# Loading the expert matrices of a hybrid decoder step as whole 4 MB transfers instead of 2 MB halves

## What is computed

```
def moe(x, w_router, b_router, w_gate, b_gate, w_up, b_up, w_down, b_down):
    logits = (x @ w_router + b_router)
    top_v, top_i = lax.top_k(logits, TOP_K)          # 4 of 32
    wts = softmax(top_v)
    ...
    g = xblk @ w_gate[eid] + b_gate[eid]
    u = xblk @ w_up[eid] + b_up[eid]
    g = minimum(g, 7.0); u = clip(u, -7.0, 7.0)
    hmid = (u + 1.0) * (g * sigmoid(1.702 * g))
    yblk = hmid @ w_down[eid] + b_down[eid]
```

## Time and profile before

| | before |
|---|---|
| device time, median of 3 runs | 1263.45 us (1262.87 to 1263.94) |
| the profiled execution's own time | 1263.72 us |
| span of its profile (first to last instruction) | 1262.0 us |
| PE busy | 1221.6 us (97%) |
| bytes moved | 455.83 MB, mean 361 GB/s |
| transfers of half matrices, 2048 KB each | 62 gate, 62 up, 62 down |

### The profile page before, as it was taken

How to read it: one execution, slowest core, us unless ns; L and a number is a source line. 1 busy time by engine, 2 the same in 40 slices (tenths; PEclk the granted TensorE clock), 3 DMA queues, 4 the chain that set the end, 5 groups by cost and what they waited for, 6 DMA issues and landing times.

```text
span 1262.0 us, 15821 instructions
## 1 busy us (share of the span) xinstructions
PE 1221.6 (97%) x6208; PEld 670.4 (53%) x6208; DVE 356.9 (28%) x958; ACT 225.9 (18%) x432; POOL 24.6 (2%) x53
## 2 busy tenths in 40 slices
PE   8999999999999999999999999999999999999998
PEld 6887778886444434354343444444343444434356
DVE  3423732236331212222121222222122231212136
ACT  2422422013111111111111101111111111111133
POOL 1000110001000000000000000000000000000000
PEclk9999999999999999999999999999999999999999
DMA  9742677745999999999999999999999999999980
GB/s 299 232 132 82 198 240 264 286 167 216 407 428 426 429 427 428 428 428 429 428 429 428 427 428 423 426 427 427 428 427 429 427 429 429 427 430 427 422 346 35
DMA packets 72668, 455.83 MB, mean 361 GB/s; under 512 B 7335, under 2 KB 41813, under 8 KB 47277
## 3 DMA queue, kind: packets, MB, share of 16 engines
q1 hardware_dynamic: 66192, 443.83, 85.7%
q0 software_dynamic: 2736, 9.08, 2.2%
q10 hardware_dynamic: 3692, 2.28, 0.7%
HBM read 449.33 MB, written 5.83 MB: 361 GB/s over the span
## 4 chain that ended last, share of the span: by engine, by line
PE 80%; DMA 16%; DVE 2%; ACT 1%; issue 0%; DVEq 0%; SPq 0%; ACTq 0%
PE bank L895 38%; PE bank L647 19%; DMA ring<-in_w_up_dram 11%; PE bank L911 5%; DMA ring<-in_w_gate_dram 5%; PE bank L930 4%; PE bank L968 3%; PE bank L1193 2%; PE bank L903 2%; PE bank L1069 2%; DVE regC L1653 1%; DVE regC L1635 1%; PE bank L689 0%; PE bank L918 0%; PE bank L786 0%
## 5 line engine op out<-in xcount | busy, mean ns | idle before, releaser
L895 PE MATMUL bank<-ring,regC 128*64 128x512 f32 x1984 | 437.8, 595 | 19.1 <-DVE regC L1653 11.3
L895 PEld LDWEIGHTS bank<-ring,regC 128*64 128x64 f32 x1984 | 138.1, 137 | 282.1 <-issue 256.2
L1635 DVE TENSOR_TENSOR regC<-bank,biasT 128x512 f32<-128x512 f32 x61 | 42.2, 692 | 591.6 <-PE bank L903 590.2
L895 PE MATMUL bank<-ring,xe_odd 128*64 128x512 f32 x896 | 198.4, 594 | 5.4 <-DMA ring<-in_w_up_dram 4.2
L647 PE MATMUL bank<-regA,ring 128*128 128x264 f32 x832 | 192.6, 388 | 0.0
L647 PEld LDWEIGHTS bank<-regA,ring 128*128 128x128 f32 x832 | 155.3, 190 | 30.8 <-issue 3.8
L895 PEld LDWEIGHTS bank<-ring,xe_odd 128*64 128x64 f32 x896 | 63.0, 137 | 128.9 <-issue 118.5
L911 PEld LDWEIGHTS bank<-regC,regB 128*128 128x128 f32 x816 | 95.9, 192 | 14.4 <-issue 13.5
L911 PE MATMUL bank<-regC,regB 128*128 128x128 f32 x816 | 100.7, 277 | 0.5 <-DVE hT L1671 0.3
L2091 ACT ACTIVATE regD<-bank 128x512 f32<-128x512 f32 x62 | 37.0, 597 | 241.5 <-PE bank L895 232.8
L1671 DVE TENSOR_TENSOR hT<-hT,bank 128x264 f32<-128x264 f32 x144 | 56.5, 426 | 74.7 <-PE bank L930 25.6
(11 more groups left out here) (346 smaller groups left out, 691.1 us busy)
## 6 DMA issues: line engine op xcount, KB each, us to landing
ring<-in_w_up_dram SPq DMA_DIRECT2D x62, 2048.0 KB, 24.8
ring<-in_w_down_dram SPq DMA_DIRECT2D x62, 2048.0 KB, 26.1
ring<-in_w_gate_dram SPq DMA_DIRECT2D x62, 2048.0 KB, 21.8
ring<-in_w_in_dram SPq DMA_DIRECT2D x28, 1024.0 KB, 7.0
out_dram<-ring POOLq DMA_DIRECT2D x9, 512.0 KB, 5.1
ring<-in_state_gla_dram POOLq DMA_DIRECT2D x8, 512.0 KB, 5.3
ring<-in_w_o_dram SPq DMA_DIRECT2D x4, 1024.0 KB, 7.5
ring<-in_w_gate_dram SPq DMA_DIRECT2D x4, 1024.0 KB, 28.7
```

The costliest lines, as they stand in the source:

```text
L895: ins = mm(bank[b][n * CAP:(n + 1) * CAP, :], lhs(k + i), by_k[s][:, i, n * 512:(n + 1) * 512], start=(k + i == 0), stop=(k + i == KT - 1))
L1635: return v.tensor_tensor(out, v_in, bias.to_broadcast([P, HALF, 2, CAP]), ALU.add)
```

## The change

For the experts at places 2 to 29 a matrix is now one transfer of 4 MB into two neighbouring slots. `by_pair` views slots 0 and 1, 2 and 3, 4 and 5, 6 and 7 as one place of two halves. SP issues it when both slots are free (it waits for one more used piece than the first half did before), and it raises the semaphore of the even slot alone. PE waits for that semaphore ahead of both pieces, so no matmul of a matrix starts before all 4 MB have landed. The experts at places 0, 1, 30 and 31 are loaded as before (`alone`). 84 transfers of 4 MB take the place of 168 of 2 MB. Each partition's 4 MB share is two runs of 16 KB, one from each half of the matrix, which lie 2 MB apart in memory.

```diff
+        by_pair = [view(ring, s * SLOT, 2, HALF * D) for s in range(0, SLOTS, 2)]
...
+        def alone(m):
+            return m < EARLY_EXPERTS * PER_EXPERT or m >= (E - (E - EARLY_EXPERTS) % UNROLL) * PER_EXPERT
+        def loader(m):
+            return m if alone(m) else m - m % 2
         def expert_loads(m):
-            return 16 * (m // SLOTS + 1)
+            m = loader(m)
+            return 16 * sum(n == loader(n) for n in range(m % SLOTS, m + 1, SLOTS))
...
+            def load_matrices(e, q, i):
+                for m in range(q * PER_EXPERT, (q + 1) * PER_EXPERT, 2):
+                    w = K3[m % PER_EXPERT // 2][0]
+                    sp.wait_ge(chunk_used, i * TURN + (m - SLOTS + 2))
+                    sp.dma_start(by_pair[m % SLOTS // 2], w[0, e].rearrange("(h p k) f -> p h (k f)", h=2, p=P))\
+                        .then_inc(slot_loaded[m % SLOTS], 16)
...
-                    load_expert(sp.value_load(order_i[0:1, bass.ds(i * UNROLL + (early + u), 1)], min_val=0, max_val=E - 1),
-                                early + u, i)
+                    load_matrices(sp.value_load(order_i[0:1, bass.ds(i * UNROLL + (early + u), 1)], min_val=0, max_val=E - 1),
+                                  early + u, i)
...
-                    return [(r % SLOTS, slot_loaded[r % SLOTS], i * loads + expert_loads(r), HALF * (r % 2))
+                    return [(r % SLOTS, slot_loaded[loader(r) % SLOTS], i * loads + expert_loads(r), HALF * (r % 2))
```

## The result

The changed kernel takes 1280.74 us (median of 4 runs, 1279.84 to 1281.61) against 1263.7 us before: 17.0 us more, a ratio of 1.0135 with a 95% interval of 1.0124 to 1.0147. Forecast were 1278.3 us and a range from 1271 to 1286.

A forecast was written before the change was run, and what follows sets the result against it. The weight stream at 428 GB/s was taken to set the expert part's time. 3.2 + 8.3 - 0.5 + 4.2 - 0.6 = +14.6 us on 1263.72 gave 1278.3 us, range 1271 to 1286.

The forecast's parts named there:

- A transfer's own cost: In the weight stream, 84 fewer transfers save between nothing and 6.7 us; 0.5 us taken for all.
- The lower bound: In the weight stream, fewer transfers save nothing, as packets fill 100.6% of sixteen engines with no rest between transfers.
- First gap: At the loop's first pair, pieces 12 and 13, the queue is empty and the later issue costs 3.2 us.
- Second gap: After the wide pass, entered 7.8 us later, the next matrix is issued too late and the stream loses 8.3 us.
- Waiting for the whole: At up of the loop's last expert, PE has both pieces to do after the pair lands: +4.2 us.
- the 0.6 made up: After the loop, PE's earlier wait of 0.56 us at 1176.84 is used up: -0.6 us.
- rival 5: TensorE's clock falls in PE's longer waits, some 6 us per pair of pieces; ten such give 1340 us; chance 3%.
- One reading of the prediction: Profile page before: DMA share 9 from eleventh slice to last but one, rate 423 to 430 GB/s from the twelfth.
- cheaper and slower transfers: Rivals on the 4 MB transfers: 0.08 us saved each, 1272.1 us, 10%; or stream 1.9% slower, 1293.9 us, 12%.
- That TensorE is the bound: Rival: TensorE bounds the kernel and the gaps vanish in its lead, 1263.7 us; chance 4%.

The follow-up runs named there:

- the two kernels with one rule each: Against the kernel before, 2 MB halves kept: issuing both when both slots are free, 1270.73 us; or PE waiting for both halves, 1273.73 us.
- the kernel with the rules alone: Against the changed kernel, two 2 MB transfers per matrix again, both issued when both slots are free, PE waiting for both halves: 1279.02 us.
- forty-two matrices that changed nothing: 4 MB transfers only at places 3 to 11 and 21 to 25, PE's program as in the kernel before: 1264.72 us, ratio 1.0004 to it.
- three matrices at place 2: 4 MB transfers only for the expert at place 2, PE's program as in the kernel before: 1266.53 us, ratio 1.0024 to it.
- the kernel with place 29 alone: Against the kernel before, 4 MB transfers only at place 29, PE waiting a second time ahead of every odd piece: 1268.61 us, ratio 1.0034.
- places 2 and 12 to 16: Against the kernel before, 4 MB transfers only there, in separate kernels, with a second PE wait ahead of odd pieces: 1270.13 and 1276.55 us.
- the four kernels that wait again ahead of every odd piece: 4 MB transfers at place 2, 12 to 16, 3 to 11 with 21 to 25, or 29, against the kernel before: 1270.13, 1276.55, 1270.17, 1268.61 us.
- the four with the same loop on SP and PE's old program: SP's loop written out; 4 MB transfers nowhere, at place 2, 12 to 16, or 3 to 11 with 21 to 25: 1264.18, 1266.53, 1272.47, 1264.72 us.
- the one with the wait rule alone: Against the kernel before, each half still issued when its slot is free, but PE waits for both halves ahead of the first piece: 1273.73 us.

## Why the prediction was right, and where its terms were off

The mechanism held at each step, and the range held the time. But every term that was off was off to the same side (by 0.5, 0.4, 0.6 and 1.7 us), so the forecast of 14.6 us was low. By the steps of the sum:

- *A transfer's own cost, 0.5 us saved.* Nothing was saved: 9.79 us a matrix against 2 x 4.90. The lower bound, no rest between queued transfers, was the true value, and a fixed part is paid only when the queue is empty: 12.9 and 13.1 us to landing at the two holes, where 12.6 was expected. With 9.79 us of moving, that is 3.1 and 3.3 us for a lone 4 MB transfer, not the 2.8 that was read from a lone 2 MB one.
- *First gap, 3.2 us.* 3.6: the issue was 0.1 later and the landing took 0.3 longer.
- *Second gap, 8.3 us.* 8.9. The wide pass began at 699.14 where 698.6 was worked out, the matrix left at 753.5 (753.0) and took 0.5 us longer to land. That it takes both rules to make this gap is shown by the two kernels with one rule each.
- *Waiting for the whole, 4.2 us; the 0.6 made up.* The 4.2 was too small by what the clock took. In the changed kernel's timeline of 1148 to 1245 the up matrix of the loop's last expert starts at 1159.66, 12.2 us after the 1147.48 of the earlier trace rows (11.0 forecast), and its second piece 5.87 us later instead of 4.2:

```profile
1159.66 5.35 PE L912 MATMUL bank<-ring,xe_odd 128*64 128x512 f32 x16 [3.24 <-DMA ring<-in_w_up_dram]
...
1165.53 3.65 PE L912 MATMUL bank<-ring,xe_odd 128*64 128x512 f32 x16
...
1230.17 7.09 PE L1086 MATMUL bank<-ring,regC 128*64 128x512 f32 x32 [1.38 <-DVE regC L1681]
```

The piece took 5.35 us instead of 3.65. The granted clock of the changed kernel around it:

```profile
1156.00:1168.00 12.00, 8.76 (x34) 2.78 (x34) 1.64 (x3) 1.23 (x2) 0.00 (x0) 0.86 0.99 423
```

That is the largest part of the sum that was missing: rival 5 named the clock, but as a case of its own with 3 in 100, and not as a term of the sum. Its idle time of 2.0 us per pair counted the transposes between up's pieces; gate's two pieces run back to back in 7.09 us, so the wait behind them is 9.79 - 7.09 = 2.7 us, and 3.24 here. Its price of tens of microseconds took ten pairs to run wholly at half clock. What the clock took is small, 5.35 - 3.65 = 1.7 us, since it came back within the piece (the transposes and the second piece behind it take their old 0.66 and 3.65); and it counts only here, where nothing behind it waits for the stream any more. It is not sure to come: with the wait of 2.70 us in the kernel with the rules alone it did not. With it, 3.6 + 8.9 - 0.3 + 4.2 + 1.7 - 0.6 = 17.5, where -0.3 is the difference between the two gaps added up (12.5) and the delay of the up matrix as PE meets it (12.2). From 1212.76 before to 1230.17 now are 17.4 us; the spans differ by 1279.8 - 1262.0 = 17.8.

One reading of the prediction is too wide, and nothing rests on it: in the earlier trace rows the DMA share is 8 and not 9 in the last slice but one, and the rate is 422 in the 38th slice and 346 in the 39th.

Of the rivals, cheaper and slower transfers are excluded by the kernel with the rules alone and by forty-two matrices that changed nothing. That TensorE is the bound, as its 97% suggested, is excluded by three matrices at place 2, which delay the end although PE first waits for a transfer at 583 us.

The Trainium skill's page "DMA: Bandwidth & Descriptors", section "Anatomy of one DMA — SWDGE (gpsimd) path", gives a transfer a fixed cost of about 2.0 us; its fit was taken with transfers that GpSimd issued, and here SP issues them. In a queue that is never empty the trace shows none of it (9.79 us against 2 x 4.90); a lone transfer of 2 MB shows 2.8. The same page of the Trainium skill, in its section "Latency and other measured facts", reports a loss for copies in which the rows of neighbouring partitions lie 2 MiB apart. The stream of this change, in which one partition's two runs lie 2 MB apart and neighbouring partitions 16 KB, stays at 428 GB/s; no run here has the layout of that section.

## What to carry to other kernels

Where a stream of transfers sets the time, look for the moments at which its queue is nearly empty; here a coarser transfer cost time there, by its later issue and by the later start of the work that frees its buffers, and at the end of the stream, where the late start of its consumer is no longer hidden. In half of all matrices, elsewhere, it cost nothing that could be told. Before merging transfers to save their fixed cost, compare landing to landing in the full queue with a lone transfer: what the full queue already hides can't be saved. A busy share of 97% on the engine that consumes the stream says little: the hole that cost half of the loss lies in 12 us in which that engine was busy throughout.

## What had not been expected of the hardware

The granted clock of TensorE fell in some waits and not in others of the same length: it fell around 532.62 and 1041.55, behind waits of 2.71 and 2.70 us (0.86 in both stretches below), and stayed at 1.00 from 580 to 690, with a wait of 2.71 us ahead of 650.11. In the kernel with the rules alone it fell behind a wait of 2.04 us (at 981.47) and not behind 2.70 (at 1157.75). The changed kernel's stretch around the first fall; from 1036 to 1048 the clock reads 0.86 as well:

```profile
528.00:540.00 12.00, 9.29 (x38) 2.92 (x36) 1.12 (x2) 0.71 (x2) 0.00 (x0) 0.86 1.01 429
```

Both falls cost nothing at the end, since PE met the stream again later (it waits for landings at 591.37 and at 1100.30). A stretch of 0.86 is a mean of the two levels, 1.00 (2.4 GHz) and 0.50 (1.2 GHz): in the kernel with place 29 alone the row from 1137.33 to 1140, behind the wait of 4.78 us, reads 0.50. Why one wait brings the fall and a longer one does not is open.

The stall behind the experts (3.94 us above, 3.9 and 4.9 in the profiles of places 2 and 12 to 16) is in the profiles of three of the four kernels that wait again ahead of every odd piece, and in none of the four with the same loop on SP and PE's old program. But more waits alone are not shown to be the cause: the kernel with the rules alone and the one with the wait rule alone have an additional wait ahead of every even piece at places 2 to 29, and their profiles show the 0.74 us of the kernel before. Why PE stalls there is open.
